# Value pages of the samples as the moving operand, four pages on four column quarters of TensorE

## The reference, cut to what matters

```python
D_MODEL, SEQ, DEPTH, DEC_BATCH, PAST_LEN, PAGE_SIZE = 1024, 1024, 2, 8, 2048, 128
N_HEADS, N_KV_HEADS, HEAD_DIM = 16, 4, 64
...
def stick_breaking_attention(q, k, v, q_off):
...
        log_between = lax.cumsum(log_keep, axis=z.ndim - 1, reverse=True) - log_keep
        w = jnp.where(past, jnp.exp(jax.nn.log_sigmoid(z) + log_between), 0.0)
        o = jnp.einsum('bngqs,bsnd->bqngd', w.astype(v.dtype), v)
...
def forgetting_attention(q, k, v, log_f, q_off):
...
        p = jax.nn.softmax(jnp.where(visible, z + decay, -jnp.inf), axis=-1)
        o = jnp.einsum('bngqs,bsnd->bqngd', p.astype(v.dtype), v)
```

## Time and profile before

| | us |
|---|---|
| median of three runs | 3202.53 |
| fastest and slowest of them | 3201.16, 3210.64 |
| the profiled execution | 3201.7 |
| its span, first to last instruction | 3199.7 |
| PE busy in the span | 3002.5 (94%) |
| DVE, ACT, POOL busy | 1401.9, 901.0, 888.6 |

### The profile page before, as it was taken

One profiled execution on the slowest core, in us unless ns is written; L12 is line 12 of the kernel. 1 busy time (PEld: TensorE's weight loads), 2 busy tenths in 40 slices (PEclk: granted clock), 3 DMA queues, 4 the chain that ended last, 5 costly groups with the idle time before them and its releaser, 6 DMA issues. The chain is left out here.

```text
span 3199.7 us, 50554 instructions
## 1 busy us (share of the span) xinstructions
PE 3002.5 (94%) x19894; PEld 2870.9 (90%) x19894; DVE 1401.9 (44%) x1823; ACT 901.0 (28%) x1229; POOL 888.6 (28%) x415
## 2 busy tenths in 40 slices
PE   6989997998999999999999899899899999999994
PEld 5978886888999999999989789788899999999994
DVE  5144445554434334334361444655443433343435
ACT  3035554443211111111230354433321121111111
POOL 2112222332122322222311244445312222222220
PEclk8989897999999999999999899999999999999997
DMA  2112211221111111111101233133111111111111
GB/s 99 55 54 65 65 41 47 83 84 53 40 40 53 47 51 47 39 39 53 54 31 48 82 102 94 56 110 106 57 40 40 40 53 53 53 39 39 40 39 53
DMA packets 177557, 182.75 MB, mean 57 GB/s; under 512 B 31927, under 2 KB 167569, under 8 KB 177334
## 3 DMA queue, kind: packets, MB, share of 16 engines
q1 hardware_dynamic: 175086, 172.14, 17.5%
q10 hardware_dynamic: 2304, 8.39, 0.8%
HBM read 171.67 MB, written 8.99 MB: 56 GB/s over the span
## 5 line engine op out<-in xcount | busy, mean ns | idle before, releaser
L334 PE MATMUL psum<-x_hi,w_hi 128*128 128x344 f32 x2688 | 578.1, 324 | 4.2 <-issue 2.7
L334 PE MATMUL psum<-x_lo,w_hi 128*128 128x344 f32 x2688 | 571.9, 321 | 0.0
L334 PE MATMUL psum<-x_hi,w_lo 128*128 128x344 f32 x2688 | 569.0, 320 | 0.0
L334 PEld LDWEIGHTS psum<-x_hi,w_hi 128*128 128x128 f32 x2688 | 451.7, 189 | 7.5 <-issue 4.7
L334 PEld LDWEIGHTS psum<-x_lo,w_hi 128*128 128x128 f32 x2688 | 456.2, 190 | 0.0
L334 PEld LDWEIGHTS psum<-x_hi,w_lo 128*128 128x128 f32 x2688 | 449.6, 188 | 0.0
L867 DVE TENSOR_TENSOR xT<-psum,xT 128x1032 f32<-128x1032 f32 x176 | 217.0, 1233 | 287.2 <-PE psum L334 287.2
L713 POOL TENSOR_TENSOR w_lo<-raw,w_hi 128x2048 fp32r<-128x2048 f32 x44 | 203.3, 4621 | 419.9 <-ACT w_hi L709 419.9
L1267 PE MATMUL psum<-wt,tokv 128*64 128x128 f32 x2304 | 319.2, 286 | 0.0
L1671 POOL TENSOR_SCALAR rows<-rows,stat 128x128 f32<-128x128 f32 (+7 forms) x128 | 220.5, 1726 | 309.8 <-DVE stat L1420 309.7
L854 POOL TENSOR_TENSOR act_lo<-gate,act_hi 128x1032 fp32r<-128x1032 f32 x44 | 106.3, 2415 | 717.5 <-ACT act_hi L825 717.5
(11 more groups left out here) (202 smaller groups left out, 4410.8 us busy)
## 6 DMA issues: line engine op xcount, KB each, us to landing
kpage<-in_cache_k_dram SPq DMA_DIRECT2D x256, 128.0 KB, 2.0
vpage<-in_cache_v_dram SPq DMA_DIRECT2D x256, 128.0 KB, 2.0
raw<-in_ffn_w_a_dram SPq DMA_DIRECT2D x22, 1024.0 KB
raw<-in_ffn_w_b_dram SPq DMA_DIRECT2D x22, 1024.0 KB
raw<-in_ffn_w_down_dram SPq DMA_DIRECT2D x22, 1024.0 KB
raw<-in_w_qkv_dram SPq DMA_DIRECT2D x10, 1024.0 KB, 4.8
ncum<-ncum_scratch ACTq DMA_DIRECT2D x16, 512.0 KB, 4.0
raw<-in_w_o_dram SPq DMA_DIRECT2D x6, 1024.0 KB, 4.9
```

The costliest lines, as they stand in the source:

```text
L334: last = nc.tensor.matmul(out[:, c, 0:NG], w[:, k, cols], r(k)[:, c * NG:(c + 1) * NG], start=(k == 0 and part == 0), stop=(k == kt - 1 an ...
```

## The change

The roles of the operands are swapped. A page now is the moving operand, all its 256 value columns at once. The stationary is 32 columns of `score`: the 16 heads of this page and of its neighbour in the pair. Its output is 32 partitions by 256 columns, and the four pages of a quad write the four quarters of the partitions of `dec`, columns 0 to 255. A quarter has 16 rows that are wanted and 16 that weigh a page with its neighbour's weights. The four quads of a sequence add up in place.

When a sequence is done, DVE copies the 128 by 256 sums to a tile `vsum` (two of them alternate), and PE multiplies each half of it with 8 columns of `pick`, a matrix of zeros and ones that adds the right 16 rows of the four quarters and drops the others; the result stands in columns 256 to 383 of `dec`, in the layout as before. `pick` is made once per layer on DVE from pieces of the identity. The gather of a sequence stands in front of the first quad of the next one, and the last one in step 128. Quads stand from step 72 on in layer 0 and from step 77 on in layer 1 (there units began at step 72); SP waits per quad.

```diff
-            V_FIRST, V_OVER = PER_TURN + 8, 54
+            V_FIRST = PER_TURN + 8
+            V_OVER = 49 if fox else 54
-            v_step = [V_FIRST + u * V_OVER // UNITS for u in range(UNITS)]
+            v_step = [STEPS - 2 - V_OVER + u * V_OVER // (UNITS // 2) for u in range(UNITS // 2)]
...
-                            sp.wait_ge(s_vu, u - V_SLOTS + 1)
+                            sp.wait_ge(s_vu, (u - V_SLOTS) // 2 + 1)
...
-                    def sum_values(u):
-                        b, n = u // SEQ_UNITS, 2 * (u % SEQ_UNITS)
-                        if u == 0:
+                    def sum_values(quad):
+                        b, n0 = quad // SEQ_QUADS, 4 * (quad % SEQ_QUADS)
+                        if quad == 0:
                             pe.wait_ge(s_ca, WEIGHED)
-                        if fox and v_step[u] == V_FIRST + 4:
-                            pe.wait_ge(s_cd, SUMS + 12)
-                        pe.wait_ge(s_vp[u % V_SLOTS], 32 * (u // V_SLOTS + 1))
+                            if fox:
+                                pe.wait_ge(s_cd, SUMS + 12)
+                        if n0 == 0 and b >= 1:
+                            gather_heads(b - 1)
+                        for u in (2 * quad, 2 * quad + 1):
+                            pe.wait_ge(s_vp[u % V_SLOTS], 32 * (u // V_SLOTS + 1))
+                        for n in range(n0, n0 + 4):
+                            q = n % 4
+                            last = nc.tensor.matmul(dec[q * 32:(q + 1) * 32, 0:KVD], score[:, b, n // 2 * 2:n // 2 * 2 + 2, :],
+                                                    vpage[(2 * quad + q // 2) % V_SLOTS][:, q % 2, :],
+                                                    start=(n0 == 0), stop=True, skip_group_check=True)
+                        last.then_inc(s_vu, 1)
+
+                    def gather_heads(b):
+                        pe.wait_ge(s_ve, b + 1)
+                        if b == 0:
+                            pe.wait_ge(s_pick, 2)
                         for hf in range(HALVES):
-                            c = (b * HALVES + hf) * HH
-                            for j in range(2):
-                                last = nc.tensor.matmul(dec[:, c:c + HH], vpage[u % V_SLOTS][:, j, hf * P:(hf + 1) * P],
-                                                        score[:, b, n + j, hf * HH:(hf + 1) * HH],
-                                                        start=(u == 0 and hf == 0 and j == 0), stop=True, skip_group_check=True)
-                        last.then_inc(s_vu, 1)
+                            c = KVD + (b * HALVES + hf) * HH
+                            last = nc.tensor.matmul(dec[:, c:c + HH], vsum[b % 2][:, hf * P:(hf + 1) * P], pick[:, hf * HH:(hf + 1) * HH],
+                                                    start=False, stop=True, skip_group_check=True)
+                        last.then_inc(s_vg, 1)
...
+                    def copy_sums(b):
+                        dve.wait_ge(s_vu, SEQ_QUADS * (b + 1))
+                        if b >= 2:
+                            dve.wait_ge(s_vg, b - 1)
+                        nc.vector.tensor_copy(vsum[b % 2][:, :], dec[:, 0:KVD]).then_inc(s_ve, 1)
...
                     def store_samples():
-                        dve.wait_ge(s_vu, UNITS)
-                        src = dec[:, 0:P]
+                        dve.wait_ge(s_vg, NB)
+                        src = dec[:, KVD:KVD + P]
...
+                    nc.vector.tensor_tensor(pick[:, :], ident[:, 0:NH], ident[:, 3 * NH:4 * NH], ALU.add)
+                    nc.vector.tensor_tensor(pick_half[:, :], ident[:, 4 * NH:5 * NH], ident[:, 7 * NH:8 * NH], ALU.add).then_inc(s_pick, 1)
...
                         if fox:
                             softmax_piece(N)
+                        for quad in units_at(v_step, N - 1):
+                            if quad % SEQ_QUADS == SEQ_QUADS - 1:
+                                copy_sums(quad // SEQ_QUADS)
                     store_samples()
```

More of the change, by code:

```diff
@@ L1065, in trunk_program @@
         UNITS = NB * NPAGE // 2
-        SEQ_UNITS = NPAGE // 2
+        SEQ_UNITS, SEQ_QUADS = NPAGE // 2, NPAGE // 4
         ROWS = 4
@@ L1109, in attention @@
             vnew = tile("vnew", [P, HALVES, NB])
+            pick, pick_half = tile("pick", [P, NH]), tile("pick_half", [P, NH])
+            vsum = [tile(f"vsum{j}", [P, KVD]) for j in range(2)]
             off[0] = TAIL
@@ L1139, in attention @@
             s_ca, s_cd, s_cp = sem(f"dc_act_{l}"), sem(f"dc_dve_{l}"), sem(f"dc_pe_{l}")
+            s_pick, s_ve, s_vg = sem(f"dc_pick_{l}"), sem(f"dc_sums_copied_{l}"), sem(f"dc_heads_{l}")
             s_vu, s_tail, s_out = sem(f"dc_used_{l}"), sem(f"dc_tail_{l}"), sem(f"dc_out_{l}")
@@ L1155, in units_at @@
             def units_at(table, N):
-                return [u for u in range(UNITS) if table[u] == N]
+                return [u for u, step in enumerate(table) if step == N]
             groups, of_step, of_unit = [], {}, {}
@@ L1350, in _ @@
                             sum_values(u)
+                        if N == STEPS:
+                            gather_heads(NB - 1)
                         if 0 <= N - CUM < 4:
@@ L1360, in _ @@
                             pe.wait_ge(s_cd, SUMS + 10)
[L1361 to L1364, removed]
+                            nc.tensor.matmul(dec[:, 2 * P:3 * P], ones[:, :], small[:, 0, :], start=True, stop=True).then_inc(s_cp, 1)
+                            nc.tensor.matmul(dec[:, 3 * P:4 * P], ones[0:1, :], score[0:1, :, NPAGE, :], start=True, stop=True)\
                                 .then_inc(s_cp, 1)
@@ L1496, in softmax_piece @@
                                                          new, ALU.mult))
+                    def copy_sums(b):
[3 more added lines that the diff above has]
+                        nc.vector.tensor_copy(vsum[b % 2][:, :], dec[:, 0:KVD]).then_inc(s_ve, 1)
                     def store_samples():
-                        dve.wait_ge(s_vu, UNITS)
-                        src = dec[:, 0:P]
+                        dve.wait_ge(s_vg, NB)
+                        src = dec[:, KVD:KVD + P]
                         if fox:
-                            step(nc.vector.tensor_tensor(small[:, 2, :], dec[:, 0:P], small[:, 2, :], ALU.add))
+                            step(nc.vector.tensor_tensor(small[:, 2, :], src, small[:, 2, :], ALU.add))
                             step(nc.vector.tensor_tensor(small[:, 2, :], small[:, 2, :], small[:, 1, :], ALU.mult))
@@ L1531, in _ @@
                     read_scores(0)
+                    dve.wait_ge(s_pick, 1)
+                    nc.vector.tensor_tensor(pick[:, :], pick[:, :], pick_half[:, :], ALU.add).then_inc(s_pick, 1)
                     low_queries(1)
```

## The result

The changed kernel takes 3145.27 us (median of four; 3142.28 to 3152.25) against 3203.92 for the kernel before: a ratio of 0.9823, 95% interval 0.9805 to 0.9841. That is 7 us under 3152, the low end of the forecast range, and three times the gain that was forecast. The profiled execution took 3142.28 us, 59.4 less than that of before.

A forecast was written before the change was run, and what follows sets the result against it. PE was taken to bound both value stretches. The terms -11.0 + 2.3 - 11.7 + 2.0 = -18.4 us took 3201.7 to 3183.3, with 0.8 for the median 3184 us; range 3152 to 3219.

The forecast's parts named there:

- five slots: Samples' value matmuls: a quad's eight records take five record times, 1.21 us a quad, 77.4 us for 64.
- the rival: Quads in both layers: the four quarters run in parallel to the end, 0.56 us a quad, about 3159 us; chance 0.18.
- The shares: Part of PE's 14.6 us saving per layer that reaches the time: 11.0 us first layer, 11.7 us second.
- The added waits: PE's gathers waiting for DVE copies: 2.3 us net at the first layer's step 78, 2.0 us in the second layer.
- What was free: DVE's copies, the selection adds, the last gather and SP's loads per quad were taken as hidden, at no cost.
- The slower case: Quads' moving streams run one at a time whatever the quarter: 1.86 us a quad, +15.3 us, 3218 us; chance 0.29.

The follow-up runs named there:

- the two orders over two quarters: Changed kernel with a quad's pages sent to quarters 0, 1, 0, 1 or 0, 0, 1, 1: 3162.47 us and, in a single run, 3164.4 us.
- the early copy: Changed kernel with the copy of a sequence's sums ahead of the query subtraction and output store in its DVE step: 3137.39 us, ratio 0.981 to before.
- the queries in the second step: Changed kernel with sums copied earlier in their DVE step and next head's queries prepared in a head's second step, both layers: 3127.65 us.
- the run with one quarter: Changed kernel with all four pages of a quad writing partitions 0 to 31: 3204.22 us, ratio 1.0016 to the kernel before.

## Why the prediction was wrong

**The step that failed** is "the second record of a quarter must wait for the first: then the first record of the next quarter starts together with the second of the one before, and five slots remain". The first half holds, two records of one quarter stand 0.216 to 0.24 apart. The second half took program order between quarters for given. The rows from which I took it had a single column group at work; they could not show it. Two slots remain, shown by the changed kernel and by the two orders over two quarters. So the term that failed is the five slots of a quad. PE's starts put a quad at 0.57 us against the 1.21 forecast; the rival's 0.56 was right in mechanism and size. I gave it 0.18.

**The shares.** With full overlap the rival had -24.9 + 2.0 for the second layer: 23.9 were measured, and POOL's product is the wait that grew (none to 8.5 us), as said, 5.8 of it on the eight-block row and the rest on shorter ones. For the first layer it had -23.1 + 2.3 and 32.5 came. The growth of PE's waits there was 3.6 us for the scan (9.2 to 12.8 in the stretch) and 4.2 for the copies, 7.8 where 12.4 + 2.3 were allowed. The other term was not in the sum at all: 22.5 us at half clock in place of 34.6, so 12.1 us at half the pace, up to 6 us. With it the sum closes: 35.5 - 7.8 + 6 = 33.7, and 32.5 were measured. In the second layer the half-speed time went the other way, 7.0 to 11.6 us. The run with the kernel before and 32 columns shows that this time moves, by 14.4 us in its one profile, where nothing but the moving side was made wider.

**The added waits.** At step 78 PE waited 3.30 us for the copy (3.4 forecast), behind the query subtraction as named; a copy takes 0.415 us (0.42). The second layer had 1.1 us (2.0 taken). Net, the early copy shows that the 3.3 us cost next to nothing, where 2.3 were charged: the chain behind it sets nearly the same end.

**What was free** stayed so. SP waits for PE just twice in the second layer's stretch now; nearly all of its 22.3 us is one wait ahead of the first quad. It issues its loads one behind the other, and PE waits for none of them. There is little room left: with the queries in the second step PE did wait once for a page, 1.7 us.

**The slower case**, no overlap, came out in the run with one quarter: PE's price as forecast (1.84 us for 1.86), but 3204 us in place of 3218. The clock makes up for it, again a term that was not in the sum: in the first layer half speed took 10.1 us in place of 34.6, so the stretch was 218.6 us, 5 under before, though PE's waits there grew from 9.2 to 11.0. The second layer was 12 us longer where 8.3 had been worked out.

## What to carry to other kernels

A record with few moving columns has a floor: here 0.112 us with 8 columns and with 32. With the operands swapped it is paid by its columns, 0.216 us for 256, and that was a gain only with several in different column quarters, which then ran side by side whatever their order in the program. Where a trace does not show how two things run together, price the best case with more than a small chance, and measure the pair by itself. When the bounding engine gets faster, the next gain is in the chain that waits once per head: here moving 2.3 us of query work out of it, in one layer only, gave another 39 us, up to half of them through a clock that stood less at half.

## What the runs showed of the hardware

Column quarters worked here as four queues: records of one quarter follow at 0.216 us for 256 f32 columns (the run with one quarter), first records of different quarters start 7 ns apart (the changed kernel) or 13 ns (quarters 0, 0, 1, 1), and in that last order an earlier matmul that waits for its quarter, 240 ns, does not hold a later one for another. Eight weight loads of 32 columns were made inside 0.2 us beside four running matmuls (the changed kernel). And in stretches where PE's value work took equally long the clock stood at half for different times: 34.6 us with 8 moving columns, 20.2 with 32 and 10.1 with quads of 256 in one quarter, one profile each; over whole executions the mean clock with 8 and with 32 columns was the same, 0.964.
